# Attention of the second block by pairs of heads in half-array tiles, with value products per query tile

## What is computed

```python
sc = jnp.einsum('bgrqd,bgcd->bgrqc', qb, kc).astype(f32) - slopes * d_c      # 31 compressed keys
p_c = jax.nn.softmax(sc, axis=-1) * (t >= CMP_LEN - 1).astype(f32)[:, None]
...
ss = jnp.einsum('bgrqd,bgqnkd->bgrqnk', qb, k_sel).astype(f32) - slopes[..., None] * d_s
...
sw = jnp.einsum('bgrqd,bgkd->bgrqk', qb, kwb).astype(f32) - slopes * d_w
...
return gb[0] * o_c + gb[1] * o_s + gb[2] * o_w
```

## Time and profile before

| | |
|---|---|
| median of 3 runs | 1934.29 us (1932.0 to 1935.02) |
| the profiled execution | 1932.1 us |
| its span, first to last instruction | 1930.3 us |
| granted TensorE clock over the span | 0.97 |
| TensorE busy (products) | 1861.3 us, 96% |
| VectorE busy | 1245.9 us, 65% |
| ACT busy | 721.7 us, 37% |
| GpSimd busy | 214.8 us, 11% |
| chain that ended last, by engine | PE 90%, DVE 4%, issue 3%, ACT 1%, DMA 1% |

### The profile page before, as it was taken

The page is one execution under the profiler, slowest core; times in us unless marked ns, Lnnn a source line. Parts: engine busy times, 40 slices in busy tenths (PEclk is TensorE's granted clock), DMA queues, the critical chain, the costliest instruction groups (busy, mean ns, idle before and its releaser), DMA issues.

```text
span 1930.3 us, 24000 instructions
## 1 busy us (share of the span) xinstructions
PE 1861.3 (96%) x8760; PEld 1500.8 (78%) x8760; DVE 1245.9 (65%) x1834; ACT 721.7 (37%) x976; POOL 214.8 (11%) x50
## 2 busy tenths in 40 slices
PE   7999999999999999999999997999899889999996
PEld 7885888888888886888888886879566668888885
DVE  5448788787875448778786877643565365445555
ACT  5323534233334233533232334463675342222221
POOL 0000000000000000000000000333100224443430
PEclk9999999999999999999999997995899999999998
DMA  6330343333332331333433333221000212223231
GB/s 251 117 105 34 119 151 109 135 126 130 120 119 74 123 101 34 121 138 109 149 112 130 130 109 117 88 88 66 23 0 1 88 44 99 97 88 107 87 109 44
DMA packets 28476, 192.60 MB, mean 100 GB/s; under 512 B 3328, under 2 KB 3712, under 8 KB 6144
## 3 DMA queue, kind: packets, MB, share of 16 engines
q1 hardware_dynamic: 22752, 156.77, 23.0%
q10 hardware_dynamic: 5664, 35.00, 5.4%
HBM read 185.47 MB, written 2.10 MB: 97 GB/s over the span
## 4 chain that ended last, share of the span: by engine, by line
PE 90%; DVE 4%; issue 3%; ACT 1%; DMA 1%; DVEq 0%; SPq 0%; ACTq 0%; PEldq 0%
PE ps L437 27%; PE ps L439 27%; PE ps L438 27%; PE ps L840 1%; PE ps L793 1%; PE ps L595 1%; PE ps L607 1%; PE ps L807 1%; PE ps L494 1%; DMA raw<-in_weights 0%; PE ps L843 0%; PE ps L486 0%; PE ps L522 0%; PE ps L507 0%; PE ps L579 0%
## 5 line engine op out<-in xcount | busy, mean ns | idle before, releaser
L437 PE MATMUL ps<-xh,wh 128*128 128x512 f32 x1504 | 595.4, 396 | 21.8 <-DVE xl L1455 10.0
L439 PE MATMUL ps<-xh,wl 128*128 128x512 f32 x1504 | 587.8, 391 | 0.0
L438 PE MATMUL ps<-xl,wh 128*128 128x512 f32 x1504 | 587.6, 391 | 0.0
L914 ACT ACTIVATE wh<-raw 128x2048 fp32r<-128x2048 f32 x144 | 275.6, 1914 | 451.5 <-DMA raw<-in_weights 449.0
L420 POOL TENSOR_TENSOR wl<-raw,wh 128x2048 fp32r<-128x2048 f32 x46 | 214.6, 4666 | 1673.6 <-ACT wh L914 1673.6
L437 PEld LDWEIGHTS ps<-xh,wh 128*128 128x128 f32 x1504 | 284.0, 189 | 87.4 <-issue 29.7
L438 PEld LDWEIGHTS ps<-xl,wh 128*128 128x128 f32 x1504 | 283.9, 189 | 60.6 <-issue 2.6
L439 PEld LDWEIGHTS ps<-xh,wl 128*128 128x128 f32 x1504 | 283.6, 189 | 59.6
L1493 DVE TENSOR_TENSOR wl<-raw,wh 128x2048 fp32r<-128x2048 f32 x98 | 223.9, 2286 | 87.4 <-ACT wh L914 87.3
L437 PE MATMUL ps<-ah,wh 128*128 128x512 f32 x608 | 239.0, 393 | 6.3 <-DVE x L1724 3.3
L439 PE MATMUL ps<-ah,wl 128*128 128x512 f32 x608 | 237.7, 391 | 0.0
(11 more groups left out here) (266 smaller groups left out, 2089.4 us busy)
## 6 DMA issues: line engine op xcount, KB each, us to landing
raw<-in_weights SPq DMA_DIRECT2D x144, 1024.0 KB, 4.8
adab<-in_ada ACTq DMA_DIRECT2D x22, 1024.0 KB, 4.8
t<-in_cst ACTq DMA_DIRECT2D x1, 3200.0 KB, 10.3
turned<-q ACTq DMA_DIRECT2D x8, 256.0 KB, 4.2
turned<-k ACTq DMA_DIRECT2D x8, 256.0 KB, 4.2
adab_tail<-in_ada ACTq DMA_DIRECT2D x2, 1024.0 KB, 8.4
out_y<-x SPq DMA_DIRECT2D x8, 256.0 KB, 2.0
raw<-in_weights SPq DMA_DIRECT2D x2, 512.0 KB, 7.2
```

The costliest lines, as they stand in the source:

```text
L437: pe.matmul(out, w_hi, m_hi, start=start, stop=False)
L438: pe.matmul(out, w_hi, m_lo, start=False, stop=False)
L439: return pe.matmul(out, w_lo, m_hi, start=False, stop=stop)
L914: act.activation(wh[:, s, :], raw[:, s, :], ACT.Copy).then_inc(hi_made, 1)
```

## The change

- Units are now pairs of heads: U = 9r + v covers head r of both groups, 36 units, all written out (no hardware loop).
- `scores`: for each group a product that contracts over 64 partitions (queries `q2[h]`, keys `ksw[h]`, h = lower or upper half), into a bank each; four banks in two sets instead of three. `qc`, its copies and its MEMSET go.
- `turn`: the transposes of both heads, into two banks (one set instead of three), so each waits for the copy of the unit before.
- `values`: per unit, right after its copy, for each key tile j and each group a product of 64 value columns with the 128 query columns of this tile; group g writes the partitions of half g. The table `plan` goes.
- ACT: one copy for both heads' transposes, one for the output of both heads.
- VectorE: one reciprocal for both heads' sums; in v = 8 one MEMSET, reduction and subtraction or multiplication for both.
- `tsl` gets two sets for r even and odd; `pb`, `pt`, `ptc`, `cst` grow for two heads, and lie at other addresses.
- The order on TensorE for each U: `turn(U)`, `scores(U + 2)`, `values(U - 1)`. On VectorE: `minima(U + 1)`, `weigh(U)`. On ACT: `exps(U + 1)`, `keep_turned(U)`.

```diff
-            def attend(r, first, last_turn):
-                def scores(U):
...
-                        pe.matmul(ps[:, U % 3, 0:w], qc[:, g, i * P:(i + 1) * P], ksw[:, v // 4, 0:w], start=True,
-                                  stop=True).then_inc(s2_done, 1)
...
-                for U in range(18):
-                    if U + 2 < 18 or not last_turn:
-                        if U + 2 in (9, 18):
-                            pe.wait_ge(staged2, 2 * r + (U + 2) // 9 + 1)
-                        scores(U + 2)
-                    if U in plan:
-                        values(r if U > 3 else r - 1, *plan[U])
-                    turn(U)
...
+            def scores(U):
+
+                r, v = divmod(U, 9)
+                if U >= 2:
+                    pe.wait_ge(sc_done, unit_signals(U - 2))
+                for i in (v % 4,) if v < 8 else range(NT):
+                    for g, h in enumerate(halves):
+                        tok = q2[h, r, i * P:(i + 1) * P]
+                        if v < 8:
+                            w = (i + 1) * P
+                            last = pe.matmul(ps[:, 2 * (U % 2) + g, 0:w], tok, ksw[h, v // 4, 0:w], start=True, stop=True)
...
+                last.then_inc(s2_done, 1)
...
+            def turn(U):
+
+                v = U % 9
+                if U:
+                    pe.wait_ge(pt_evac, U)
+                for g in range(2):
+                    pe.wait_ge(p_ready, unit_signals(U) - (1 - g if v < 8 else 0))
...
+                last.then_inc(t_done, 1)
...
+            def values(U):
+
+                r, v = divmod(U, 9)
+                pe.wait_ge(pt_evac, U + 1)
...
+                for j in range(i + 1) if v < 8 else (0,):
+                    for g, h in enumerate(halves):
+                        if v < 8:
+                            last = pe.matmul(ps[h, 6 + r % 2, i * P:(i + 1) * P], vv[:, j, b * P + HD * g:b * P + HD * g + HD],
+                                             pt[:, U % 2, g, j, :], start=(v == 0), stop=False)
...
+            scores(0)
+            scores(1)
+            for U in range(UNITS):
+                turn(U)
+                if U + 2 < UNITS:
+                    scores(U + 2)
+                if U:
+                    values(U - 1)
+            values(UNITS - 1)
...
+            def minima(U):
+
+                r, v = divmod(U, 9)
+                dve.wait_ge(s2_done, U + 1)
...
+            def weigh(U):
+
+                r, v = divmod(U, 9)
+                dve.wait_ge(exp_done, unit_signals(U))
+                if v < 8:
+                    w = (v % 4 + 1) * P
+                    dve.reciprocal(soft[:, 2, 2 * v:2 * v + 2], soft[:, 1, 2 * v:2 * v + 2]).then_inc(rs_ready, 1)
...
+            minima(0)
+            for U in range(UNITS):
+                if U + 1 < UNITS:
+                    minima(U + 1)
+                weigh(U)
```

More of the change, by code:

```diff
@@ L380, in build, with unit_signals @@
         mean_bank = (3, 3, 3, 2)
+        halves = (slice(0, HD), slice(HD, P))
+        UNITS = 4 * 9
+        def unit_signals(U):
+            return U // 9 * 17 + min(2 * (U % 9 + 1), 17)
         @block.sync
@@ L795, in scores @@
                     else:
                         for i in range(NT):
[L797 to L812, removed]
@@ L833, in values @@
[L833 to L845, removed]
@@ L1317, in head_out, with stage @@
-            def head_out(r, g):
-                h = slice(HD * g, HD * g + HD)
-                act.wait_ge(values_used, r * 6 + 3 * g + 6)
-                act.activation(cols(att_f[h, :], r * S, S), ps[h, 6 + g, :], ACT.Copy).then_inc(att_evac, 1)
-            stage(0, 0)
-            attend(0, True, False)
-            with act.Fori(1, 3) as r:
-                attend(r, False, False)
-            attend(3, False, True)
-            head_out(3, 1)
-            past(act, att_evac, 8)
+            def stage(r):
+                for g in range(2):
+                    act.activation(tsl[:, r % 2, g, :], alibi, ACT.Copy, scale=slopes[:, r + 4 * g:r + 4 * g + 1]).then_inc(staged2, 1)
@@ new lines, in exps @@
+            def exps(U):
+                v = U % 9
+                if v < 8:
+                    w = (v % 4 + 1) * P
+                    for g in range(2):
+                        act.wait_ge(sc_done, unit_signals(U) - (1 - g))
+                        at = 2 * v + g
+                        act.activation(pb[:, U % 3, g, 0:w], pb[:, U % 3, g, 0:w], ACT.Exp, bias=soft[:, 0, at:at + 1], scale=-1.0,
+                                       accum_out=soft[:, 1, at:at + 1]).then_inc(exp_done, 1)
+                else:
+                    act.wait_ge(sc_done, unit_signals(U))
+                    act.activation(pb[:, U % 3, :, 0:P], pb[:, U % 3, :, 0:P], ACT.Exp, scale=-1.0).then_inc(exp_done, 1)
@@ new lines, in heads_out @@
+            def heads_out(r):
+                act.wait_ge(values_used, 9 * r + 9)
+                act.activation(att[:, r, :], bank(6 + r % 2), ACT.Copy).then_inc(att_evac, 1)
+            stage(0)
+            exps(0)
+            for U in range(UNITS):
+                r, v = divmod(U, 9)
+                if U + 1 < UNITS:
+                    exps(U + 1)
+                keep_turned(U)
+                if U == 3:
+                    after(CMP0 + 3)
+                if v == 4 and r < 3:
+                    stage(r + 1)
+                if v == 2 and r:
+                    heads_out(r - 1)
@@ L1331, in _ @@
+            heads_out(3)
+            act.wait_ge(att_evac, 4)
             for i in range(4):
```

222 lines of the change are left out of this document (80 added, 142 removed).

## The result

The changed kernel takes 1954.05 us (median of 6 runs, 1947.92 to 1958.48), the kernel before 1934.53 us beside it (6 runs, 1931.78 to 1935.28). The ratio is 1.0101, 95% interval 1.0078 to 1.0124: 1% slower. The forecast was 1950.

What follows compares the result with a forecast made beforehand. TensorE bounds the stage before; after, VectorE in series with its return through TensorE. Stage 138 us against 125.5 (plus 12.8), plus 3 for the clock, makes 16 more: 1950 us, range 1930 to 1976.

Steps and rivals of the forecast that it cites:

- The return: VectorE's minima wait for scores queued behind turn on TensorE: 0.56 + 0.107n + 0.213m us, n tiles turned, m scored.
- The predicted view of the chain: Profile's chain through the second block's attention stage: VectorE, transposes, scores, VectorE by turns, no longer TensorE alone.
- VectorE's own work: VectorE's operations in the stage, without waits: 19.8 us a pair of heads, 79 us for four.
- The stage at full clock: Second block's attention: four pairs 130 us, plus start, end and stall, 138 us against 125.5 before.
- The clock: TensorE's granted clock in the stage: two units of 36 at the low level, 3 us added.
- rival 1: Clock low for a third to all of the stage, 12 to 36 units at 1.4 us more: 1964 to 1998 us; chance 0.20.
- Behind the stage: After the second block's attention: slab products begin at the last product as before, memory places change no transfer; nothing added.
- TensorE's sum: TensorE's work in the stage: 21 us a pair including 27 changes of form at 0.2, 84 us for four.
- Rival 4: TensorE stays the stage's bound and VectorE keeps up: stage 92 us, kernel 1901 us; chance 0.04.
- Half tiles side by side: Two heads' half-array products on TensorE run concurrently: a group costs 2.13 us plus 0.2, instead of 4.3.
- ACT at nothing: ACT's copies and exponentials in the stage only shrink and aren't on the path: costed at nothing.
- The stall of 3.4 us: VectorE's scaling slowed beside GpSimd's weight-slab subtraction at the fourth unit: 3.77 us instead of 0.35, staying after the change.

Runs made afterwards that it cites:

- e3: Changed kernel plus 26 unread products of 256 or 512 columns on TensorE behind the values, to hold the clock: 1948.77 us, ratio 1.0084.
- e8: Changed kernel with scores(U + 2) issued ahead of turn(U), plus 1984 unused bytes that restore the second MLP's activation addresses of the kernel before: 1907.92 us.
- e9: e8 with ACT's split of a weight slab, and GpSimd's subtraction behind it, moved from the fourth unit to the thirty-fifth: 1901.7 us, ratio 0.9835.
- e5: Changed kernel with scores issued ahead of turn, its halves run one after the other instead of side by side: 1936.68 us, ratio 1.0019.
- e7: Changed kernel with ACT's shared copy of the transposes undone, two copies in each of 32 units: 1956.53 us.

## Why the prediction was right, and where it was not

**The return, the deciding step: right.** The place (VectorE's minima), the cause (the order) and the size were as written. At full clock the timelines have 1.29 us for n = 1 and m = 3 and 1.61 for n = 2 and m = 4 (after), 1.75 for n = 3 and the compressed scores (e3, and after at 1462.36 us), and 1.23 for n = 4 and m = 1 (e3, and after at 1466.51); the formula gives 1.31, 1.62, 1.71 and 1.20. A row of after, and two of e3:

```profile
1419.90 0.55 DVE L1892 CUSTOM_DVE_ANT_0 pb<-ps,tsl 128x384 f32<-128x384 f32 x1 [1.29 <-issue]
```
```profile
1422.91 0.27 DVE L1907 MEMSET pb<- 128x256 f32 x1 [1.75 <-PE ps L803]
...
1427.05 0.28 DVE L1902 CUSTOM_DVE_ANT_0 pb<-ps,tsl 128x128 f32<-128x128 f32 x1 [1.23 <-issue]
```

In e3 each pair of heads has 14.0 us in which VectorE doesn't work, where the sum had 12.7; the added products stand ahead of some transposes there and are part of it. In after it waited 65.6 us for its minima, over the "50 us in all" of the prediction, since half of the stage ran at the lower level.

**The predicted view of the chain: half right.** The return appears in it as "issue", not as transposes and scores. Of 28 waits the releaser wasn't inferred. Of the other signs, TensorE is busy for 0.73 of the stage, as predicted (under 0.75). A pair of heads takes 35.0, 33.4 and 33.3 us from compressed unit to compressed unit (32 to 34 predicted), and the stage of the profiled execution, the slowest of six, 147.2 (134 to 145).

**VectorE's own work: 79 us predicted, too high by some 10.** A pair takes 17.2 us of work, not 19.8. The failed term is the reciprocal: "0.32 (it waits for its own result)" came from the earlier trace rows, at 1397.58 and 1398.54 us, which stand in the hardware loop over r = 1, 2. In the straight code of r = 3, in the same kernel, the same two operations are 0.19 apart:

```profile
1463.35 0.15 DVE L1938 RECIPROCAL soft<-soft 128x1 f32<-128x1 f32 x1
1463.54 0.55 DVE L1940 TENSOR_SCALAR pb<-pb,soft,gates 128x512 f32<-128x512 f32 x1
```

Only in the loop has the scaling a "[0.16 <-DVE soft L1938]"; the straight code of r = 0 has 0.19 too (1360.79 to 1360.98 us). After has no loop: 32 times 0.13 us, 4.2 us, and the edit that the prediction costed at nothing ("registers and branches of the hardware loop go") had a price after all. The second MEMSET, which runs beside the minimum (0.06 us, 32 times, 1.9 us), scalings that follow each other 0.03 us sooner (0.25 us for 128 columns, not 0.28) and a compressed unit of 3.1 us and not 3.4 are most of the rest.

**The stage at full clock: 138 us predicted.** Four pairs at 31.25 and 8.3 for start, stall and end make 133 us; no execution of after ran there at full clock, so this is worked out, not measured. 5 us too high.

**The clock: 3 us predicted, several times that.** This is the term that was mis-sized. The mechanism (a thin load, the return doubled) was there, and the price of 1.4 us a unit is near the one unit that can be compared (3.25 against 1.75 us); that it would be two units of 36 was not. In the profiled execution PEclk of 0.76 makes 71 us of 147 at the lower level. From that execution to the 133 us are 14 us. So one of the prediction's own signs of being wrong came ("the granted clock is 0.50 for long"), and with it the condition of rival 1, a third or more of the stage. Its time, 1964 us and up, didn't come, because the stage at full clock was shorter than reckoned and because the 71 us at the lower level cost 14 us, where 14 units of 3.5 + 1.4 us, as the prediction reckons, would make 20 (an estimate). The choice leaned on one stretch, 2.27 us busy of 5 at full clock, ahead of the fall. After has the same two-sided picture, 2.83 us of 5 busy at full clock and 3.44 at the lower:

```profile
1410.00:1415.00 5.00, 2.83 (x26) 1.53 (x22) 3.19 (x17) 3.10 (x8) 0.00 (x0) 1.00 0.00 0
...
1430.00:1435.00 5.00, 3.44 (x20) 2.91 (x22) 2.51 (x12) 1.82 (x4) 0.00 (x0) 0.50 0.00 0
```

A single stretch in which the clock held said little on how long it would hold. It is also what makes after's times spread over 10 us, where e8's agree within 0.3.

**Behind the stage: 0 predicted, 3.5 measured.** "Memory places change no transfer" was beside the point: they change the rate of products.

So that 1950 came out as near to 1954 as it did is in part luck: the errors have opposite signs. The full-clock work was 5 us too high, the time behind the stage 3.5 too low, and the clock some 11 too low in the profiled execution. In the median, 4.4 us under that execution, it was some 7, if all of the difference is the stage's clock (an estimate).

**TensorE's sum: near.** 84 us was the sum for TensorE as the bound, with 0.2 us for each of 27 changes of form a pair; in e9 TensorE is busy for 84.0 us. Rival 4 made of the 84 a stage of 92 us, of which 3.4 were the stall, and a kernel of 1901 us. Without the stall that is 89, and e9 has 93.3 and 1901.7. The Trainium skill ("TensorEngine Tiling (Array Packing)", section Tiling Modes: a switch drains the array) gives no size for it; here, from the start of four transposes to that of the scores behind them are 1422.22 - 1421.62 = 0.60 us, of which 0.43 are passes, so 0.17. (By its own term of 0.23 in each of 36 returns, free switches would take some 8 us off the prediction's total, not "some 4".) The gain of its section Overview, up to 2 times, is there for the products: four passes take 1.13 us in two halves and 1.98 in one (e5). Rival 4 was wrong on this order and near on these tiles.

**The rest.** Half tiles side by side: right (e5). ACT at nothing: right (e7). The stall of 3.4 us: there, but smaller, 2.5 us in the profiled execution of after (two scalings of 256 columns in 3.23 us instead of 0.74), and removable (e9).

## What to carry to other kernels

When an engine that is short becomes faster, draw the loop through all engines in their issue order: a consumer that waits for a product queued behind the wait for that consumer's own last result pays the whole way through the other engine each time. Issue the work that doesn't depend on the late operand ahead of the wait; two exchanged lines were worth 45 us of 1954. And read a duration from the same kind of code in which it will be used, in a loop or out of it, and a clock from many stretches, not from the one in which it held.

## What the runs showed of the hardware that was not expected

- A wait on VectorE for its own last result costs 0.13 us more in a loop in hardware (0.32 us from reciprocal to scaling) than in straight code (0.19). In the loop the value waited for is computed from the loop's variable; whether that or the loop itself costs the time, no run separates.
- Products of 128x512 follow each other at 100 / 443 = 0.226 us or 100 / 440 = 0.227 us counted over the stretch, by the addresses of the activations alone. In the trace the first of three products with these activations has a mean of 394 ns in after and 389 in e8:

```profile
L442 PE MATMUL ps<-ah,wh 128*128 128x512 f32 x147 | 58.0, 394 | 0.0
```
```profile
L443 PE MATMUL ps<-ah,wh 128*128 128x512 f32 x151 | 58.7, 389 | 0.0
```

- In a chain in which VectorE and TensorE wait for each other, one more step on TensorE and a lower clock add to each other: with the values in the return the stage took 208 us at a granted clock of 0.56, without them 147 at 0.76.
